# A two-block transformer kernel: the last weight tile of each norm taken by halves of the columns, and its turns moved

## What is computed

```python
for l in range(2):
    h = layer_norm(ALPHA * h + 0.5 * swiglu(h, gate1, up1, down1))   # norm (0, l)
    h = layer_norm(ALPHA * h + mix(h @ w_in) @ w_out)                # norm (1, l)
    h = layer_norm(ALPHA * h + cross_attn(h, mem, q, k, v, o))       # norm (2, l)
    h = layer_norm(ALPHA * h + 0.5 * swiglu(h, gate2, up2, down2))   # norm (3, l)
h = layer_norm_2(A2 * h + y(h @ w_in_2) @ w_out_2)                   # norm ("A",)
h = layer_norm_2(A2 * h + moe(h))
h = h + sigmoid(h @ w_ple_gate + b) * (p @ w_ple)
```

## Time and profile before

| | |
|---|---|
| median of three runs | 2451.29 us (2451.28 to 2451.35) |
| the profiled execution, its span | 2450.9 us |
| instructions | 32509 |
| HBM read | 662.50 MB |

### The profile page before, as it was taken

One profiled execution on the slowest core, in us unless ns is written; L12 is line 12 of the kernel. 1 busy time (PEld: TensorE's weight loads), 2 busy tenths in 40 slices (PEclk: granted clock), 3 DMA queues, 4 the chain that ended last, 5 costly groups with the idle time before them and its releaser, 6 DMA issues.

```text
span 2450.9 us, 32509 instructions
## 1 busy us (share of the span) xinstructions
PE 2371.4 (97%) x13087; PEld 1623.3 (66%) x13087; DVE 1164.6 (48%) x1599; ACT 805.2 (33%) x1010; POOL 195.7 (8%) x94
## 2 busy tenths in 40 slices
PE   8999999999999999999999999999999999999998
PEld 7889988888888998888898974333333333333334
DVE  5567856755755785675585843211111211111114
ACT  4454344544444434454447322111111111111111
POOL 0002402200200250220020100000000000000000
PEclk9999999999999999999999999999999999999999
DMA  7664453556556545355545559999999999999994
GB/s 247 214 206 158 152 182 125 178 190 201 172 189 206 162 148 187 124 179 190 196 138 191 161 215 385 426 427 426 428 427 427 428 426 427 426 427 428 427 427 180
DMA packets 223800, 665.07 MB, mean 271 GB/s; under 512 B 9889, under 2 KB 164511, under 8 KB 191056
## 3 DMA queue, kind: packets, MB, share of 16 engines
q1 hardware_dynamic: 223696, 663.57, 71.4%
HBM read 662.50 MB, written 1.05 MB: 271 GB/s over the span
## 4 chain that ended last, share of the span: by engine, by line
PE 74%; DMA 18%; DVE 4%; ACT 3%; issue 1%; SPq 0%; DVEq 0%; ACTq 0%
PE ps L683 18%; DMA ring<-in_w_up_dram 17%; PE ps L694 13%; PE ps L668 10%; PE ps L1262 9%; PE ps L1306 6%; PE ps L767 3%; PE ps L876 2%; PE ps L1244 2%; PE ps L1235 2%; PE ps L1403 1%; PE ps L1284 1%; PE ps L1117 1%; PE ps L928 1%; PE ps L729 1%
## 5 line engine op out<-in xcount | busy, mean ns | idle before, releaser
L2013 DVE TENSOR_TENSOR ring_halves<-ring,ring_halves 128x2048 fp32r<-128x2048 f32 x206 | 511.4, 2490 | 201.3 <-ACT ring_halves L1485 200.8
L683 PE MATMUL ps<-x_halves,ring_halves 128*128 128x512 f32 (+1 forms) x2560 | 457.9, 340 | 2.8 <-issue 2.8
L683 PEld LDWEIGHTS ps<-x_halves,ring_halves 128*128 128x128 f32 x2560 | 394.6, 189 | 62.7 <-issue 3.7
L1485 ACT CAST ring_halves<-ring 128x2048 fp32r<-128x2048 f32 x206 | 392.3, 1908 | 131.2 <-PE ps L694 101.0
L1262 PE MATMUL ps<-ring,work 128*64 128x512 f32 x1536 | 344.0, 595 | 41.8 <-DMA ring<-in_w_up_dram 41.1
L2537 DVE TENSOR_SCALAR work<-work 128x128 f32<-128x128 f32 x64 | 19.3, 344 | 692.2 <-PE ps L1262 692.2
L694 PE MATMUL ps<-ring_halves,work_halves 128*128 128x512 f32 x1184 | 288.9, 391 | 0.2
L1262 PEld LDWEIGHTS ps<-ring,work 128*64 128x64 f32 x1536 | 106.6, 137 | 272.3 <-issue 195.0
L694 PEld LDWEIGHTS ps<-ring_halves,work_halves 128*128 128x128 f32 x1184 | 221.6, 188 | 47.0 <-issue 2.3
L668 PE MATMUL ps<-x_halves,ring_halves 128*128 128x256 f32 x2016 | 251.4, 286 | 0.0
L668 PEld LDWEIGHTS ps<-x_halves,ring_halves 128*128 128x128 f32 x2016 | 245.6, 193 | 1.1 <-issue 0.6
(11 more groups left out here) (277 smaller groups left out, 2166.5 us busy)
## 6 DMA issues: line engine op xcount, KB each, us to landing
ring<-in_w_up_dram SPq DMA_DIRECT2D x96, 2048.0 KB, 37.0
ring<-in_w_down_dram SPq DMA_DIRECT2D x33, 2048.0 KB, 37.0
work<-in_w_up_dram SPq DMA_DIRECT2D x32, 2048.0 KB, 35.5
work<-in_w_down_dram SPq DMA_DIRECT2D x31, 2048.0 KB, 40.0
ring<-in_w_in_dram SPq DMA_DIRECT2D x52, 1024.0 KB, 5.2
ring<-in_ffn_gate_dram SPq DMA_DIRECT2D x44, 1024.0 KB, 5.4
ring<-in_ffn_up_dram SPq DMA_DIRECT2D x44, 1024.0 KB, 5.4
ring<-in_ffn_down_dram SPq DMA_DIRECT2D x44, 1024.0 KB, 4.9
```

The lines of the kernel that those rows point to most:

```text
L683: mm = pe.matmul(out, wt[:, o:o + P], x, start=(k == 0 and n == 0), stop=(k == DT - 1 and n == 1))
L1485: nc.scalar.copy(high_of(name)[:], ring[:, s, :]).then_inc(hi_done.add(name), 1)
L2013: v.tensor_tensor(ring_halves[s][:], ring[:, s, :], high_of(name)[:].bitcast(F32), ALU.subtract)\
```

## The change

For the last of the three weight tiles in each norm's tail, TensorE now takes half 0 of the columns for both `kk` and then half 1, with an event ("half", tag, t) in between, for both token tiles. The first turn stands ahead of this tile of the second token tile, where it stood in its middle. In `first_pair` the second turn stands between tiles a and b, where it stood in the middle of b's first half. VectorE adds and takes statistics for one half before it waits for the other; its `x_low` of the first token tile stands behind the second tile's normalise. ScalarE casts one weight tile between the first turn and the second root where it cast two, and the other one behind the root. In norm "A" tail and VectorE change in the same way; its second turn stays.

```diff
@@ tail
+                def last_part(name, lhs, t):
+                    for half in range(2):
+                        for kk in range(2):
+                            mm = rows_part(name, lhs, kk, t, stop=(kk == 1), halves_of=(half,))
+                        if half == 0:
+                            full(mm, ("half", tag, t))
+                    return mm
+
                 for i, (name, lhs, ready) in enumerate(parts):
                     pe.wait_ge(lo_done.sem, lo_done.at(name))
                     ready()
+                    if i == 2:
+                        full(last_part(name, lhs, 0), ("t0", tag))
+                        break
                     for kk in range(2):
-                        mm = rows_part(name, lhs, kk, 0, stop=(i == 2 and kk == 1))
-                full(mm, ("t0", tag))
+                        rows_part(name, lhs, kk, 0)
                 for i, (name, lhs, ready) in enumerate(parts):
+                    if i == 2:
+                        transposes(tag, 0, hn)
+                        release(last_part(name, lhs, 1), name)
+                        break
                     for kk in range(2):
-                        if (i, kk) == (2, 1):
-                            transposes(tag, 0, hn)
-                        mm = rows_part(name, lhs, kk, 1, stop=(i == 2 and kk == 1))
+                        mm = rows_part(name, lhs, kk, 1)
                     release(mm, name)
@@ first_pair
                 half(a_name, a_bank, 0, (0, 1))
+                transposes(tag, 1, hn)
                 open_bank(b_bank, b_name)
                 arrived(b_name)
-                half(b_name, b_bank, 0, (0,))
-                transposes(tag, 1, hn)
-                half(b_name, b_bank, 0, (1,))
+                half(b_name, b_bank, 0, (0, 1))
@@ norm "A"
+            def w2o_last(t):
+                for half in range(2):
+                    for kk in range(2):
+                        mm = w2o_part(3, kk, t, (half,))
+                    if half == 0:
+                        full(mm, ("half", after, t))
+                return mm
...
+            transposes(after, 0, hn)
+            release(w2o_last(1), "w2o3")
@@ ScalarE, ln
+                    if t == 1 and tag[0] != "A":
+                        next_high(parts[1])
                     evac_T(tag, t, gname, i)
                     if tag[0] != "A":
                         x_high(tag, t)
-                        for name in (parts[:2] if t == 0 else parts[2:]):
-                            next_high(name)
+                        next_high(parts[0 if t == 0 else 2])
@@ VectorE, ln
                 for t in range(TT):
-                    if t == 0:
-                        pe_group(("t0", tag))
-                    else:
-                        slot_used(dve, parts[2])
                     for half in range(2):
+                        if half == 0:
+                            pe_group(("half", tag, t))
+                        elif t == 0:
+                            pe_group(("t0", tag))
+                        else:
+                            slot_used(dve, parts[2])
                         c = slice(half * 512, half * 512 + 512)
                         v.scalar_tensor_tensor(out=hn[:, t, c], in0=h[:, t, c], scalar=alpha,
                                                in1=ps[:, 4 + 2 * t + half, :], op0=ALU.mult, op1=ALU.add)\
                             .then_inc(emptied[4 + 2 * t + half].sem, 1)
-                    for half in range(2):
                         bank_empty(4 + 2 * t + half, acc_name(tag))
-                        ins = v.bn_stats(stat[:, t, half, :], hn[:, t, half * 512:half * 512 + 512])
+                        ins = v.bn_stats(stat[:, t, half, :], hn[:, t, c])
...
                     normalise_rows(tag, t)
...
+                    if t == 1 and tag[0] != "A":
+                        x_low(tag, 0)
                     evac_T(tag, t, gname, i)
-                    if tag[0] != "A":
-                        x_low(tag, t)
+                if tag[0] != "A":
+                    x_low(tag, 1)
```

More of the change, by code:

```diff
@@ L685, in by_columns_wide, with rows_part @@
                 release(mm, name)
-            def rows_part(name, lhs, kk, t, start=False, stop=False):
+            def rows_part(name, lhs, kk, t, start=False, stop=False, halves_of=(0, 1)):
                 high, low = high_of(name), ring_halves[slot_of[name]]
                 x_high, x_low = lhs(kk, t)
-                for half in range(2):
+                for half in halves_of:
                     o = kk * D + half * 512
@@ L1112, in _, with w2o_part @@
             by_columns("ma3", 1)
-            def w2o_part(j, kk, t):
+            def w2o_part(j, kk, t, halves_of=(0, 1)):
                 s = slot_of[f"w2o{j}"]
-                for half in range(2):
+                for half in halves_of:
                     mm = pe.matmul(ps[:, 4 + 2 * t + half, :], yT[:, 2 * j + kk, t * P:t * P + P],
@@ L1133, in _ @@
             after = ("A",)
-            for j in (1, 2, 3):
+            def w2o_last(t):
[5 more added lines that the diff above has]
+                return mm
+            for j in (1, 2):
                 y_part(j)
                 for kk in range(2):
-                    mm = w2o_part(j, kk, 0)
-            full(mm, ("t0", after))
-            for j in (1, 2, 3):
+                    w2o_part(j, kk, 0)
+            y_part(3)
+            full(w2o_last(0), ("t0", after))
+            for j in (1, 2):
                 for kk in range(2):
-                    if (j, kk) == (3, 1):
-                        transposes(after, 0, hn)
                     mm = w2o_part(j, kk, 1)
                 release(mm, f"w2o{j}")
+            transposes(after, 0, hn)
+            release(w2o_last(1), "w2o3")
             def router(t):
```

## The result

The change makes the kernel faster by 15.4 us: 2435.9 us median (2434.9 to 2437.6, 4 runs) against 2451.3, a ratio of 0.9938 with a 95% interval of 0.9926 to 0.9950. A later series gave 0.9941 (0.9927 to 0.9954) for the same kernel. The profiled execution spans 2433.1 us, where that of before spans 2450.9. The two spans lie 17.8 us apart, more than the medians: a run's time is 1.7 to 1.9 us above its own span wherever both are on record (2434.9 beside 2433.1), so the profiled execution of before, 2452.7 by this estimate, was 1.4 us slower than the median of its runs, and that of after 1.0 faster than its own.

What follows compares the result with a forecast made beforehand. TensorE, busy 97%, bounds the kernel before the experts, weight loads bound the experts; norms 9.6 plus third wait 3.3 make 12.9 off 2450.9, so 2438.0 profiled and 2438.4 us median, 8-in-10 range 2434.5 to 2445.

Steps and rivals of the forecast that it cites:

- The norms: At eight norms the waits at both turns go, so line 683 starts 1.20 us earlier each, 9.6 us together.
- The first turn's cover: Twelve matmuls instead of six hide the first turn's copies before line 767; its 0.58 us wait goes, 0.8 to spare.
- the second wait: TensorE's wait at the second turn for the second token tile's normalised rows, 0.62 us per norm, would go.
- just in time: ScalarE's cast ahead of the second root would end at 432.8, the root being due at 432.88.
- the slower rival: In eight norms ScalarE's cast ahead of the root comes late, by 3.7 us giving 2464.6 us; chance 0.04.
- z: Lateness of ScalarE's cast ahead of the root; the second turn waits z - 0.42, a net loss from 2.0 us on.
- The third wait: At line 683 after three norms, TensorE's wait for VectorE's late product would go: 3 x 1.09 = 3.3 us.
- Norm A: The ninth norm, in fp32: its second turn already starts without a wait, so 0, between -0.3 and +0.3 us.
- the increments: Two more event increments in each of nine norms: taken as 0, though the skill's figure would add 0.5 us.
- The clock: TensorE's granted clock, 0.51 between 1357.40 and 1364.30 after 2.62 us idle, would still fall, sliding by 9 to 13 us.
- the clock rival: The granted clock does not fall behind TensorE's longest wait: 3.0 us less, 2435.4 us; chance 0.14.
- swallowed: Rival at the experts: their weight stream does not start earlier, so nothing is seen, 2451 us; chance 0.05.

Runs made afterwards that it cites:

- both chains: Kernel before with VectorE's x_low of the first token tile behind the second normalise and ScalarE's second cast behind the root: 2448.11 us, ratio 0.9987.

## Why the prediction was right, and where it was off

**The norms: 9.6 predicted, 10.2 found.** The first turn's cover held. From its start to line 767 the prediction had 3.61 us (427.34 to 430.95), the trace has 3.60 (424.17 to 427.77). Root behind the first turn: 5.54 predicted, 5.50 found. The turn took its rows 0.70 after the second normalise's start in before (436.80 to 437.50); by that they were ready at 430.89, 0.45 before the second turn at 431.34, where 0.42 was predicted. The missing 0.08 per norm is spacing: the 96 records at 432.22 take 10.64 to line 683, 0.1108 each, not 0.1115, and the eight transposes ahead of them 0.88, not 0.90. The 0.1115 spread one gap over 80 records: in the starts of single records the 18th of them comes 0.185 behind the 17th, where all others are 0.111 to 0.113 apart. The run with both chains has this gap too, though its turn had not waited, and the 96 records of the kernel after and of the turns alone have none; why is open. A second such gap, 0.184, stands behind the first of the 48 records, so these should have ended 0.07 later than the prediction's 436.88, and the second wait was overrated by it (0.54, not 0.62). The place of the first turn was worth more than its 0.58.

**What the prediction did not see** is how the parts hang together. It said of the cast that it is "just in time", which the trace bears out (427.73 + 1.90 against the root at 429.67, and VectorE's aggregation ends at the same 429.63), but it never asked what the cast's old place costs. Its formula for the slower rival would have told: a late cast costs z - 0.42 per norm. With both casts ahead the root stood 7.17 behind the first turn (429.38 to 436.55) and not 5.50, so z is 1.67 and the formula gives 1.25; 1.21 was found, 9.7 us for eight. The agreement is close for a formula that was set up for another case, a cast whose slot comes late. The expectation for x_low alone failed by the same oversight: it took the root as bound by the aggregation, with the casts ending only 0.32 before it in the earlier trace rows.

**The third wait: 3.3 predicted, 3.5 found.** The product is done at 447.83 and TensorE ends the first tile at 442.86 + 5.73 = 448.59: 0.76 of slack, 0.8 predicted. The undersized term is the mean of the waits, 1.09 for each place where the records moved 1.18.

**Norm A and the increments: nothing, as said.** At "A" the records moved 0.13. From the first turn to line 779 the kernel after takes 3.60 with the new event in its 12 matmuls; the run with the turns alone, which has the same 12 without it, takes 3.61 (427.78 to 431.39). Of the Trainium skill's 26.3 ns per increment, which it gives for packed tiles ("TensorE: Matmul & The Clock Gate", "The cost: per-tile semaphore tail") no trace here shows anything inside such a stream.

**The clock: the step that failed.** The forecast let the wait bring the fall with it. In the profile after it did not. The profiled execution was forecast at 2438.0 and spans 2433.1: of the 4.9 between, 2.8 are the clock, 0.8 the norms and the third wait (13.7 against 12.9), 0.6 a shorter first stage, and 0.7 small pieces. The prediction priced the missing fall at 3.0. But the second profile of before shows that the fall can be missing without the change, so the clock rival was near in its number (2435.4, where the median came out at 2435.9) and unproven in its cause; part of that nearness is luck. The Trainium skill ("TensorE: Matmul & The Clock Gate", "HAM oscillation — how this bites in real kernels") tells of a clock that falls behind waits for DMA of 3 to 5 us; here a fall came with a wait of 2.6 us in seven profiles of eleven and stayed away in four. The prediction had no term for what differs between executions. Of the 2.5 us by which the median lies below the forecast, 0.8 are the norms and the third wait; where the other 1.7 come from is open. They may be what the executions differ by, but no run shows that the mix differs between the two kernels.

**Carried through.** The expert loads start earlier by what TensorE gained, and their stream is unchanged (427 GB/s), so nothing was swallowed. The fall among the experts was swallowed: the records moved from 17.25 early to 15.61 and were at 17.42 by 1829 us, since the weights bound that stage. That the medians differ by 15.2 and 15.4 us, and the change's own places by 13.7, is within the intervals (11 to 18 us) and not settled further.

## What to carry to other kernels

Before an edit takes an instruction out of one engine's way, list every chain that ends at the same event and by how much each is later than the next: here the casts ended only 0.32 us ahead of the aggregation, so that an edit paid 0.25 per norm alone and 0.56 with one cast moved too, and that cast's place carried 1.21 of the 1.28 us per norm. Parts of such a change can be worth little or less than nothing alone (turns 0.36 lost, x_low 0.25 gained), and others half of it or more when they are left out (halves 0.63, first turn's place 0.77, the cast 1.21), so test them both ways. What x_low and the second turn's place are worth when left out of the whole was not run. Moving a wait off an engine helps only if the work behind it shrinks: the scan in pieces gave back further on what it saved.

## What the runs showed of the hardware

**TensorE at half its rate at the start.** In some executions the first matmuls of the first stage take twice as long. The stage's 64 records in the first profile of before and in the second, then the stretch from 12 to 14 us in the first and in the second (6 matmuls, not 11):

```profile
10.12 14.05 PE L791 MATMUL ps<-hT,ring 128*128 128x256 f32 x64 [1.09 <-DVE hT L2027]
```

```profile
10.06 16.02 PE L791 MATMUL ps<-hT,ring 128*128 128x256 f32 x64 [1.09 <-DMA ring<-in_ffn_gate_dram]
```

```profile
12.00:14.00 2.00, 2.00 (x11) 1.77 (x10) 0.99 (x1) 0.00 (x0) 0.00 (x0) 1.00 1.10 348
```

```profile
12.00:14.00 2.00, 2.00 (x6) 1.59 (x5) 0.93 (x1) 0.00 (x0) 0.00 (x0) 1.00 1.10 349
```

The 1.00 in both stretches is no measurement: the trace's first record of the granted clock starts at 9.17 us in the first profile and at 14.05 us in the second, and the view shows 1.00 for time without a record. In the second profile the records stand 0.427 us apart until 14.03 and 0.216 from 14.26 on; in the first they are 0.216 apart from the second on. So these matmuls run at the lower level (1.2 GHz) until the clock is granted in full. All twelve profiles fit: where that first record starts at 7.9 to 9.3 us, ahead of the stage, the stage takes 14.05; in the five where it starts at 13.3 to 14.6 us, it takes 15.7 to 16.2. In both profiles of before TensorE had done the same until 9 us, 16 transposes from 5.3 us on; why the clock rises 5 us later in some executions is open.

This costs about 2 us. With the falls of the granted clock (about 1.3 or 2.8 us in the scan's stage, 1.6 among the experts) this is as much as single runs of one kernel scatter here (before: 2449.0 to 2454.1).

**A fall of the granted clock without a long wait.** At 1496.24 in the kernel after it went to the 1.2 GHz level while TensorE had no idle row since 1488; in nine of the twelve profiles such a fall stands at that place of the expert stage (1496 to 1513 us), five of them with a fall in the scan's stage as well.
